# Seven products of sums in place of eight block products, in the query, key and gate projections of the first mixer

## The reference, cut to what matters

```python
h = rms_norm(x, norm_g[0])                  # 512 x 1024
proj = h @ a_w_in                           # 1024 x 4096
q, k, v, gate = jnp.split(proj, 4, axis=-1) # 16 heads of 64
# 2-D neighbourhood attention of q, k, v with a bias table, then
return (o * jax.nn.silu(gate)) @ w_out
```

## Time and profile before

| what | us |
|---|---|
| runs | 1197.37, 1195.59, 1196.95; median 1196.95 |
| span of the profiled execution, first to last instruction | 1194.2 |
| v stage, first matmul of half 9 to first of half 0 | 39.69 to 73.89 |
| q, k and gate stage, on PE | 73.89 to 208.37 |
| first DVE instruction of the attention's `frontA` | 210.05 |
| PE busy, share of the span | 95% |

### The profile page before, as it was taken

One profiled execution on the slowest core, in us unless ns is written; L12 is line 12 of the kernel. 1 busy time (PEld: TensorE's weight loads), 2 busy tenths in 40 slices (PEclk: granted clock), 3 DMA queues, 4 the chain that ended last, 5 costly groups with the idle time before them and its releaser, 6 DMA issues.

```text
span 1194.2 us, 24820 instructions
## 1 busy us (share of the span) xinstructions
PE 1136.4 (95%) x10359; PEld 953.4 (80%) x10359; DVE 588.2 (49%) x1304; ACT 516.5 (43%) x1041; POOL 417.7 (35%) x363
## 2 busy tenths in 40 slices
PE   3999999899999999999999999998999999999996
PEld 2988888799998998656699999876777887687863
DVE  5000001862427247788623338118865896335546
ACT  4232222973424432498734356244873522133321
POOL 5734574776335446300253335230014350000000
PEclk9999999999999999999999999989999999999998
DMA  7432342323221323200032224342002232100001
GB/s 219 147 104 74 106 115 96 98 73 82 73 87 54 107 71 106 71 1 2 5 138 72 72 71 148 120 131 63 2 2 71 71 106 89 54 22 4 3 3 71
DMA packets 73337, 89.60 MB, mean 75 GB/s; under 512 B 2017, under 2 KB 66666, under 8 KB 73098
## 3 DMA queue, kind: packets, MB, share of 16 engines
q1 hardware_dynamic: 70136, 78.12, 20.4%
q0 software_dynamic: 2416, 8.26, 2.8%
q10 hardware_dynamic: 674, 1.64, 0.5%
HBM read 83.75 MB, written 4.26 MB: 74 GB/s over the span
## 4 chain that ended last, share of the span: by engine, by line
PE 83%; DVE 8%; ACT 5%; issue 2%; POOL 1%; DMA 1%; ACTq 1%; DVEq 0%; POOLq 0%
PE bank L477 76%; PE bank L804 2%; ACT arena L1380 2%; PE bank L1003 1%; POOL ring_parts L2699 1%; PE bank L714 1%; ACT arena L1496 1%; PE bank L569 1%; ACT arena L1761 1%; DVE arena L1933 1%; DMA vrow<-in_final_norm_g 1%; DVE stat L1922 1%; DVE arena L2426 0%; ACT ring_parts L1409 0%; ACTq L1375 0%
## 5 line engine op out<-in xcount | busy, mean ns | idle before, releaser
L2699 POOL TENSOR_TENSOR ring_parts<-ring,ring_parts 128x512 fp32r<-128x512 f32 (+1 forms) x236 | 309.2, 1342 | 431.1 <-ACT ring_parts L1409 339.5
L477 PE MATMUL bank<-ring_parts,arena_parts 128*128 128x256 f32 x1856 | 320.4, 282 | 0.0
L477 PEld LDWEIGHTS bank<-ring_parts,arena_parts 128*128 128x128 f32 x1856 | 269.9, 189 | 1.6 <-issue 1.2
L477 PE MATMUL bank<-hT_parts,ring_parts 128*128 128x512 f32 x704 | 235.4, 396 | 0.0
L477 PE MATMUL bank<-arena_parts,ring_parts 128*128 128x512 f32 x640 | 225.3, 402 | 2.8 <-POOL ring_parts L2699 2.8
L477 PE MATMUL bank<-ring_parts,hT_parts 128*128 128x256 f32 x1024 | 219.9, 282 | 3.8 <-POOL ring_parts L2699 2.9
L1380 ACT ACTIVATE arena<-bank 128x512 f32<-128x512 f32 (+5 forms) x295 | 139.8, 541 | 189.5 <-PE bank L477 185.6
L477 PE MATMUL bank<-arena 64*64 64x64 f32 (+7 forms) x2288 | 177.4, 301 | 7.2 <-ACT arena L1380 2.4
L477 PEld LDWEIGHTS bank<-ring_parts,hT_parts 128*128 128x128 f32 x1024 | 169.4, 189 | 5.0 <-POOL ring_parts L2699 3.7
L477 PEld LDWEIGHTS bank<-arena 128*64 128x64 f32 (+3 forms) x2288 | 119.7, 145 | 53.0 <-issue 19.4
L477 PEld LDWEIGHTS bank<-hT_parts,ring_parts 128*128 128x128 f32 x704 | 133.5, 190 | 32.0
(11 more groups left out here) (273 smaller groups left out, 1397.5 us busy)
## 6 DMA issues: line engine op xcount, KB each, us to landing
ring<-in_a_w_in SPq DMA_DIRECT2D x16, 1024.0 KB, 5.5
ring<-in_w_in SPq DMA_DIRECT2D x15, 1024.0 KB, 5.5
ring<-in_b_w_in SPq DMA_DIRECT2D x10, 1024.0 KB, 5.2
ring<-in_ple_w_gate SPq DMA_DIRECT2D x8, 1024.0 KB, 5.1
arena<-rpb_rows POOLq DMA_DIRECT2D x16, 256.0 KB, 3.6
ring<-in_a_w_out SPq DMA_DIRECT2D x4, 1024.0 KB, 5.1
ring<-in_b_w_out SPq DMA_DIRECT2D x4, 1024.0 KB, 5.0
ring<-in_w_out SPq DMA_DIRECT2D x4, 1024.0 KB, 5.2
```

Of the source, the lines that this page charges most:

```text
L477: return nc.tensor.matmul(o, l, r, start=start, stop=stop)
L2699: nc.gpsimd.tensor_tensor(rounded(r), r, read_back(high_slot(n)[:, o:o + m // 4]), ALU.subtract)\
```

## The change

The twelve halves of q, k and gate (`SEVEN`) are no longer computed as 2x2x2 blocks (two halves of the 1024 inputs, two of the 256 outputs, two of the 512 tokens), but with seven products of sums of blocks, each of 12 matmuls of 256 columns.

- Three sums of token blocks (T1, T2, T4, each 128x1024) and a fourth in place (T3) are made by DVE straight after the token norm. Their high parts are ACT's (`high_sum`), their low parts POOL's (T1, T2, T4, between `lower(2)` and the bias of head 0) and DVE's (T3). They lie in the space of x, which SP loads again after the stage.
- Per half, DVE makes four sums of weight blocks of 128x512 (`sum_operand`) and two of the seven low parts (`low_operand`), ACT seven high parts of 128x512 (`high_operand`), POOL five low parts of 128x512.
- A ring of `NOP` = 6 operand pairs takes the place of the raw slot 3 and the two high slots; the raw ring has three slots in this stage.
- The outputs are combined on the way out of PSUM: per half, ACT copies two (`first_out`, `left_out`) and DVE makes four or five `scalar_tensor_tensor` from a bank and an SBUF tile (`second_out`, `third_out`, `last_out`). PE reuses a bank for products 4, 5 and 6, and product 5 waits for `third_out`.
- `lower(3)` moves behind the bias of heads 0 and 1; `lower` of `("AO", 0)` moves to head 8, into the attention stage; the high parts of `("AO", 0)` and `("AO", 1)` move from before the attention stage into its steps 1 and 2.
- Two small loads into `wa` move from POOL's start to behind `low_pair(0, 7)`.

```diff
 # tensor engine
-            for n in AORD:
+            for n in AORD[0:4]:
                 need3(("A", n))
...
+            def seventh(m, b, again=False):
+                h, q = divmod(m, 7)
+                if q in (4, 5):
+                    pe.wait_ge(S("A_low_v"), 2 * h + q - 3)
                 else:
-                    for s in range(2):
-                        fm3(("A", n, s), "a" if n < 8 else "v", ("A", n), s * P, act)
+                    pe.wait_ge(S("A_low_g"), 5 * h + min(q, 4) + 1)
+                left, right = (tuple(rounded(v) for v in pair) for pair in (operand(m), RIGHT[q]))
+                def one(a, c, k, st, sp):
+                    return nc.tensor.matmul(b[:, 0:256], left[a][:, k, :], right[c][:, k, :], start=st, stop=sp,
+                                            skip_group_check=again)
+                for k in range(4):
+                    one(0, 0, k, k == 0 and not again, False)
+                    one(0, 1, k, False, False)
+                    ins = one(1, 0, k, False, k == 3)
+                return ins
...
+            pe.wait_ge(S("A_tlow"), 3)
+            for h, n in enumerate(SEVEN):
...
+                end(seventh(m + 2, b6), ("A", n, "6"))
...
+                end(seventh(m + 3, b7), ("A", n, "7"))
+                evacuated(pe, ("A", n, "1"))
+                end(seventh(m + 4, b1, True), ("A", n, "11"))
+                evacuated(pe, ("A", n, "7"))
+                end(seventh(m + 5, b7, True), ("A", n, "21"))
+                pe.wait_ge(S("A_22"), h + 1)
+                end(seventh(m + 6, b5, True), ("A", n, "12"))
 # scalar engine
+            def high_operand(m):
+                h, q = divmod(m, 7)
+                if q in (1, 2, 3, 6):
+                    act.wait_ge(S("A_sum"), 4 * h + min(q, 4))
+                else:
+                    raw_here(act, first7 + h)
+                free_operand(act, m)
+                nc.scalar.activation(rounded(operand(m)[0]), source(m), ACT.Copy).then_inc(S("A_high"), 1)
...
+            high_operand(0)
+            high_operand(1)
...
+            for m in range(1, 7 * len(SEVEN) + 2):
+                h, q = divmod(m - 1, 7)
+                if q == 0 and h < len(SEVEN):
+                    first_out(h)
+                if q == 0 and h:
+                    tanh_a(h - 1, 1)
+                if q == 1 and h:
+                    tanh_a(h - 1, 0)
+                if q == 4:
+                    left_out(h)
+                if m + NOP - 1 < 7 * len(SEVEN):
+                    high_operand(m + NOP - 1)
...
-            high(HI[("AO", 1)])
...
                 if 1 <= j < 9:
                     ptA_copy(j - 1)
+                if j in (1, 2):
+                    high(HI[("AO", j - 1)])
 # vector engine
+            TT(T1[1], h_block(0, 1), h_block(0, 0), ALU.subtract).then_inc(S("A_tsum"), 1)
+            dve.wait_ge(S("A_tsum"), 1)
+            TT(T2[1], h_block(1, 1), T1[1], ALU.subtract).then_inc(S("A_tsum"), 1)
+            dve.wait_ge(S("A_tsum"), 2)
+            TT(T4[1], h_block(1, 0), T2[1], ALU.subtract).then_inc(S("A_tsum"), 1)
+            dve.wait_ge(S("lo_norm0"), 8)
+            TT(h_block(0, 1), h_block(1, 1), h_block(0, 1), ALU.subtract).then_inc(S("A_tsum"), 1)
...
+                if q == 1:
+                    raw_here(dve, first7 + h)
+                    s1 = weight_block(h, 0, 1)
+                    TT(s1, s1, weight_block(h, 1, 1), ALU.add).then_inc(S("A_sum"), 1)
+                    dve.wait_ge(S("A_sum"), 4 * h + 1)
...
+                    TT(s2_sum, s1, weight_block(h, 0, 0), ALU.subtract).then_inc(S("A_sum"), 1)
+                if q in (3, 6):
+                    free_operand(dve, m)
+                    dve.wait_ge(S("A_sum"), 4 * h + 2)
+                    TT(operand(m)[1], weight_block(h, 1, int(q == 3)), s2_sum, ALU.subtract).then_inc(S("A_sum"), 1)
...
+            def prepare(m):
+                sum_operand(m)
+                low_operand(m - 1)
...
+            for m in range(1, 7 * len(SEVEN) + 3):
+                h, q = divmod(m - 1, 7)
+                if q == 2:
+                    second_out(h)
+                if q == 3:
+                    third_out(h)
+                if q == 5:
+                    last_out(h, "21")
+                if q == 6:
+                    last_out(h, "12")
+                if m + NOP - 1 < 7 * len(SEVEN):
+                    prepare(m + NOP - 1)
...
+                if q == 0 and h:
+                    gate_a(h - 1, 1)
+                if q == 1 and h:
+                    gate_a(h - 1, 0)
 # gpsimd
-            lower(2, HI[("A", 12)])
+            lower(2)
+            for n, t in enumerate((T1, T2, T4)):
+                pool.wait_ge(S("A_thigh"), n + 1)
+                pool.wait_ge(S("A_tsum"), min(n + 2, 3))
+                nc.gpsimd.tensor_tensor(rounded(t[1]), t[1], read_back(t[0]), ALU.subtract).then_inc(S("A_tlow"), 1)
...
             for h in range(16):
                 if h == 2:
-                    lower(HI[("A", 12)] + 1)
+                    lower(3)
                 if h == 4:
-                    lower(HI[("A", 12)] + 2, HI[("AO", 0)])
+                    for m in range(7 * len(SEVEN)):
+                        if m % 7 not in (4, 5):
+                            pool.wait_ge(S("A_high"), m + 1)
+                            hi, lo = operand(m)
+                            nc.gpsimd.tensor_tensor(rounded(lo), source(m), read_back(hi), ALU.subtract)\
+                                .then_inc(S("A_low_g"), 1)
+                if h == 8:
+                    lower(HI[("AO", 0)])
 # sync engine
+                if n == HI[("AO", 3)]:
+                    sp.wait_ge(filled, J[("A", SEVEN[-1], "12")] + 1)
...
+                if n == HI[("AO", 3)]:
+                    for l in range(NT):
+                        sp.dma_start(x[:, l, :], A["x"][0].rearrange("(r c) d -> c r d", r=GR)[CT * l:CT * l + CT])\
+                          .then_inc(s_x[l], 16)
```

More of the change, by code:

```diff
@@ L47 @@
 NRAW, NHI = 4, 2
+NRAW7 = 3
+NOP = 6
 CH = 64
@@ new lines, in first_out, with left_out @@
+            def first_out(h):
+                n = SEVEN[h]
+                key = ("A", n, "1")
+                b = take(act, key)
+                if h >= 2:
+                    evacuated(act, ("A", SEVEN[h - 2], "21"))
+                give(copy(sums[:, h % 2, 0, :], b[:, 0:256], 0.125 if n < 4 else 1.0), key)
+            def left_out(h):
+                n = SEVEN[h]
+                key = ("A", n, "11")
+                b = take(act, key)
+                if n < 4:
+                    copy(qT[:, 2 * n, 0:192], b[:, 64:256], 0.125)
+                    give(copy(qT[:, 2 * n, 448:512], b[:, 0:64], 0.125), key)
+                elif n < 8:
+                    give(copy(kT[:, 2 * n - 8, 0:256], b[:, 0:256]), key)
+                else:
+                    give(copy(G[:, 2 * n - 24, 0:256], b[:, 0:256]), key)
@@ new lines, in _ @@
+            high_operand(0)
+            high_operand(1)
+            act.wait_ge(filled, half_last[3] + 1)
+            high_operand(2)
+            act.wait_ge(S("A_tsum"), 4)
+            nc.scalar.activation(rounded(T3[0]), block4(h_full, 0, 1, 256), ACT.Copy).then_inc(S("A_thigh3"), 1)
+            for m in range(3, NOP):
+                high_operand(m)
+            for m in range(1, 7 * len(SEVEN) + 2):
[10 more added lines that the diff above has]
+                    high_operand(m + NOP - 1)
@@ L1487, in expA @@
+            tanh_a(len(SEVEN) - 1, 0)
             def expA(j):
@@ L1986, in _, with h_block @@
             gain_tile("norm0", 3)
[L1988 to L1994 removed]
+            def h_block(kh, t):
+                return block4(h_full, kh, t, 256)
+            evacuated(dve, ("norm0", 3, 1))
@@ new lines, in low_operand, with second_out @@
+            def low_operand(m):
+                h, q = divmod(m, 7)
+                if q in (4, 5):
+                    dve.wait_ge(S("A_high"), m + 1)
+                    hi, lo = operand(m)
+                    TT(rounded(lo), source(m), read_back(hi), ALU.subtract).then_inc(S("A_low_v"), 1)
+            def second_out(h):
+                n = SEVEN[h]
+                key = ("A", n, "6")
+                b = take(dve, key)
+                evacuated(dve, ("A", n, "1"))
+                give(STT(sums[:, h % 2, 1, :], b[:, 0:256], 0.125 if n < 4 else 1.0, sums[:, h % 2, 0, :],
+                         ALU.mult, ALU.add), key)
+                evacuated(dve, key)
@@ new lines, in third_out, with last_out @@
+            def third_out(h):
+                n = SEVEN[h]
+                key = ("A", n, "7")
+                b = take(dve, key)
+                u = sums[:, h % 2, 0, :]
+                give(STT(u, b[:, 0:256], 0.125 if n < 4 else 1.0, sums[:, h % 2, 1, :], ALU.mult, ALU.add), key)
+                evacuated(dve, key)
+                out_a(n, 1, bank[slot[("A", n, "12")]], u, 256, 512).then_inc(S("A_22"), 1)
+            def last_out(h, name):
+                n = SEVEN[h]
```

(7 more changed lines are left out.)

181 lines of the change are left out of this document (136 added, 45 removed).

## The result

| | before | after |
|---|---|---|
| median of the runs, us | 1196.42 (4 runs, 1195.59 to 1197.37) | 1217.34 (4 runs, 1215.70 to 1217.97) |
| ratio, 95% interval | | 1.0168, 1.0153 to 1.0183 |
| span of the profiled execution | 1194.2 | 1215.9 |

The kernel is 1.7% slower; the forecast was 1206.0 with a range to 1213. The direction was right, the size was not. In spans, 12.7 us more were lost than the +9.0 forecast (1203.2 against 1215.9), and I look for them stage by stage.

The account below looks back on a forecast made before the run. PE, busy 95% of the span, was taken as the bound. A gain of -15.1 us and costs elsewhere summed to +9.0 on a span of 1194.2: 1203.2, plus 2.75 for the median, 1206.0 us; range 1196 to 1213.

Parts of the forecast that it names:

- The token sums, +3.6: After the token norm, DVE's sums and POOL's low parts hold each other up, making half 9 3.6 us later.
- The wait into the first product: PE stands from the last v matmul until drain, high part and low part are through: +2.5 us, bounds 2.2 and 2.9.
- The stall of each half: PE waits 0.6 us before product 5 for `third_out`, 0.85 in two gate halves; together +7.1 us, bounds 0 and 13.
- no exclusion: Rival: DVE and POOL don't hinder one another; 3.6, 2.5 (ring start) and 7.1 vanish, 1192.8 us; chance 0.13.
- the path is the bound: Product stage: DVE and POOL's shared path sets the pace, a half over 11 us; clock or path, 1208 to 1215, chance 0.23.
- ACT's high parts, +3.0: Two ACT high parts of 1.90 us enter attention steps 1 and 2, delaying PE by 3.0 us, seen at `scoresA(4)`.
- Half 11, +4.3: In the v stage, `lower(3)` stands behind POOL's token low parts and two biases: +4.3 us, bounds 3.3 and 5.3.
- PE's gain, -15.1: Product stage: 84 matmuls of 256 columns replace 48 of 512 per half, 9.94 for 11.20 us, over twelve halves.
- The start of the ring, +2.5: First 10 us of products: ACT, POOL and DVE fill an empty ring, delaying early products; +2.5 us, bounds 0 and 3.5.
- I take +1.0 us for both, bounds 0 and 3.5: Attention: POOL's four low parts before head 8, and bias loads slowed by the reload of x, cost 1.0 us together.
- Later stages, 0: From the end of attention to the end of the kernel: no change forecast, 0 us.
- PE's clock falls: Rival: idle times halve PE's clock, costing about 3 us each; 1209, with two 1212; clock or shared path, chance 0.23.

Follow-up runs that it names:

- experiment 5: Changed kernel, but DVE makes the token sums only after POOL has finished half 9's low parts, `lower(1)`: 1216.26 us, ratio 1.0166.
- experiment 7: Changed kernel, but POOL makes only a quarter of the low part of each half's operand 0: 1210.57 us, ratio 1.0114.
- experiment 6: Changed kernel, but DVE makes s1 and s2, the next half's sums, behind `third_out` and not ahead of it: 1208.78 us, ratio 1.0103.
- experiment 3: Changed kernel with the reload of x later and the output projection's first low parts behind all heads: 1212.02 us, ratio 1.0129.
- Experiment 9: Changed kernel with the moves of experiments 1, 2, 4, 5 and 6, and ACT's two high parts in steps 6 and 9: 1195.99 us against 1197.72 before.
- experiment 1: Changed kernel, but the reload of x waits for the transposes of step 6 in the attention stage: 1211.3 us, ratio 1.013.
- experiment 4: Changed kernel, but POOL makes half 11's low parts, `lower(3)`, ahead of the bias of heads 0 and 1: 1211.3 us, ratio 1.0127.
- experiments 2 and 3: Experiment 2: changed kernel, but POOL makes the output projection's first low parts behind head 15's bias, 1212.35 us, ratio 1.0129. Experiment 3 has its own line.
- experiment 10: Experiment 9's kernel, but `lower(2)` waits for DVE's first three token sums and head 3's bias moves inside the products: 1196.97 us against 1197.72 before.

## Why the prediction was right or wrong

**Right, shown.** The token sums, +3.6: measured 3.62, of which 0.3 is a later start of everything before them (POOL's low parts at 31.87 for 31.54); experiment 5 takes the rest out. The wait into the first product: 2.43 recorded for 2.5 (2.7 by the pace of the matmuls, 84.88 - 70.82 - 11.36).

The stall of each half: the order of instructions came out as written, s2 1.67 us for "about 1.7". With 10.08 as the free pace, the eleven halves from the first product 5 (95.11) to the last (212.99) hold 117.88 - 110.88 = 7.0 us of stall; the recorded idle times in them are 5.0, and the other 2.0 stand in no recorded idle time. The forecast's 7.1 counts the first half too, so 6.5 of it belong to these eleven: eight halves lost 0.58 each for 0.6, the two with gate products 1.1 each for 0.85, the last 0.1 for nothing. That the totals agree to 0.1 us is in part luck.

The rival "no exclusion" is out (in experiment 7 s2 falls from 1669 to 832 ns by median with most of one POOL instruction gone, and a half from 10.65 to 10.08), and so is "the path is the bound": a half is 10.65, not over 11, and in experiment 6 the same instructions of DVE and POOL fit into 10.08. POOL's low part that meets a sum of 128x512 takes 1754 ns by median, the others 1298: a sum costs it 0.46 us, near the 0.5 of the earlier trace rows. That agreement is better than its reading was: POOL's four low parts at 383.86 met not only the two low parts of DVE but also short DVE instructions with two SBUF inputs behind them (one of 128x256 took 1.49 us at 387.32, and 0.41 when it came again at 390.35), so the row does not price one low part by itself.

**ACT's high parts, +3.0: 2.7.** The sign that the forecast named is there: `scoresA(4)` starts 24.7 us after `identb` (242.51) where it was about 22.0, and experiment 3, without the two loads on POOL, still has a stage 2.7 longer. Experiment 9, with the high parts in other steps, brings that start to about 23.0, and the 1.0 us left there goes with the lower clock.

**Half 11, +4.3: measured 4.7.** The forecast had POOL's `lower(2)` at 5.06. DVE's s1 and s2 of the first half start as soon as their weights are there, at 45.49, and met it: 5.78. A term left out, 0.7. The three token low parts took 7.1 for 7.5, which gave 0.4 back, and the forecast's own terms add up to 4.5 (70.5 - 66.0) and not 4.3.

**PE's gain, -15.1: mis-sized, measured -13.4.** I took 84 x 0.1183 from the v stage, 1.42 us a product. Experiments 6 and 7 show a half without waits at 10.08, 1.44 a product: 12 x (11.20 - 10.08) = 13.4. The small loss comes twelve times and is 1.7 us.

**The start of the ring, +2.5 and the first half's 0.6: measured 3.0.** From 84.88 to 95.11 are 10.23 us for five products, 7.2 without waits. The end of the stage, +0.1: 0.4, on DVE. The gain (1.7), the stall of the later halves (0.5) and the end (0.3), less 0.1 here, make the 2.4 us by which the product stage missed.

**The step that failed: in the attention, "I take +1.0 us for both, bounds 0 and 3.5".** Measured 6.7 (74.4 - 67.7). I had seen both loads on POOL, its lack of spare time, and the reload that could slow the bias loads. I priced only the low parts, at 2 us (experiment 1 leaves 2.1), let exp and transposes hide most of that, and gave the delayed load nothing. The load for one head took 8.9 us from issue to use (223.03 to 231.89) where the page had 3.6 from issue to landing; POOL stood 5.03; the low parts took 5.16; that is 10.2 us of an engine without spare time. With one of the two, attention is 69.4 to 69.8, with both 74.4, with none 67.7. So about 3 us of the first 5 are hidden and none of the second. What hides them (the four bias tiles, the banks of the scores) is argued, not shown.

Four other traces have both loads and no edit of their own in this stage (experiments 4 to 7), but POOL waits for the load more or less long. The shortest wait and the longest (experiments 6 and 7):

```profile
224.54 0.86 POOL L3047 TENSOR_TENSOR arena<-arena,cst 128x256 f32<-128x256 f32 x1 [3.37 <-DMA arena<-rpb_rows]
```
```profile
228.91 0.85 POOL L3045 TENSOR_TENSOR arena<-arena,cst 128x256 f32<-128x256 f32 x1 [5.48 <-DMA arena<-rpb_rows]
```

With waits of 3.37, 4.38, 4.73, 5.03 and 5.48 us (experiments 6, 5, 4, the changed kernel, 7) the stage takes 72.8, 73.9, 74.1, 74.4 and 74.9: each us of POOL's wait is one us of the stage. The chain of the changed kernel's attention says the same. It lies on POOL and its loads from here until 262.6, and in experiment 3, as before the change, no row of POOL is in it:

```profile
238.38 5.16 POOL ring_parts L2971 x4
```

A fall of PE's clock is a rival here, since the granted clock was 0.50 from 251 to 254, behind the waits of 1.29 and 2.32 us. It costs nothing that shows: in experiment 6 the clock stayed at 1.00 through the stage, and its point lies on the same line. The upper bound of 3.5 was the real mistake: it should have been the whole 10.2 less what is hidden. With 1.0 in place of the 6.7, the time would have been 1211.6, inside the range.

**Later stages, 0: measured +4.3, not settled.** The code there is the same, and so is PE's idle time to within 2 us. Windows of the two kernels from the attention's end to the last instruction:

```profile
292.20:1215.90 923.70, 887.42 (x8698) 737.07 (x8696) 520.43 (x1068) 402.27 (x796) 251.42 (x189) 0.99 0.20 63
```
```profile
274.80:1194.20 919.40, 885.10 (x8698) 736.05 (x8696) 519.21 (x1068) 402.23 (x796) 251.00 (x189) 0.99 0.20 64
```

The first figures are the window's length and PE's busy time: of the 4.3 us, 2.3 are PE being busy longer on the same matmuls, 2.0 idle time. In the ten experiments, which share this code, the same stretch takes 919.4 to 924.2 us. The changed kernel and its ten experiments average 921.9, so about 1.8 of the 4.3 is the scatter of one execution against another; the other 2.5 rest on a single trace of before, the equal of the lowest of the eleven. Clock falls at other places go with the scatter: what the granted clock lacked of 1.00, summed over windows of 5 us, comes to 9.8 us in the traces of 919.4 and 920.2 and to 16.3 in that of 924.2. But it is 12.1 before and 13.2 after, so it explains about 1 us between these two. One wait is longer in all eleven: PE's for the load of `cmp_w_v`, 1.2 to 1.8 us for 0.8 before. The rest stays open.

**The clock.** The rival "PE's clock falls" did happen behind half 9's wait of 3.95 us, as these windows of the changed kernel (length, busy times of PE, PEld, DVE, ACT, POOL, granted clock) show:

```profile
44.00:45.00 1.00, 1.00 (x7) 1.00 (x7) 0.00 (x0) 0.00 (x0) 1.00 (x4) 0.50 0.69 209
...
40.00:50.00 10.00, 6.69 (x33) 6.69 (x34) 3.03 (x2) 2.75 (x3) 9.98 (x14) 0.66 0.69 225
...
80.00:90.00 10.00, 7.17 (x57) 6.62 (x55) 5.29 (x4) 4.75 (x10) 6.45 (x4) 1.00 0.00 0
```

In windows of 1 us the granted clock is 1.00 to 42, 0.76 in 42 to 43, 0.50 from 43 to 49, 0.82 in 49 to 50 and 1.00 from there; the 0.66 over the ten us is their mean. A granted 0.5 in the stage was one of the signs that would have made the forecast wrong. It came in the v stage and not in the products, where every window of ten us from 80 to 210 shows 1.00, and it was swallowed by half 11's wait for POOL, as the forecast said of such a fall. The other kind, behind half 11's wait, is missing from the changed kernel's trace but stands in those of experiments 2 and 3 (0.50 in 73 to 75 and from 71.5 to 77), whose first product starts 1.6 and 3.4 us later with the same code up to there.

## What to carry to other kernels

When work moves into a stage whose queue is already the tight one, sum what it adds (issue, the time of a load beside the heaviest transfers, here 8.9 us from issue to use, instructions) and take all of it as the upper bound; two delays that each cost little alone, here 2.1 and 1.7 us, can cost much more together, here 6.7. In an in-order queue, put the instruction that frees another engine's bank ahead of preparations for later work: here that order alone took 7.0 us out of a stage of 133. A saving on the busiest engine of 13.4 us was only level with the kernel before when five such orders were mended; with a sixth it was worth 0.17% (interval 0.04 to 0.3).

## What the hardware did that was not expected

A DVE instruction with two SBUF inputs, 1.22 us alone, took 9.00 to 9.03 us in three kernels while POOL ran five instructions without a pause, and POOL was not slowed at all; with POOL held back it took 1.22. In the changed kernel three sums of the same kind took 2.19 to 2.31 us beside POOL, whose `lower(1)` took 6.34 for 5.01: both engines lost time there. Which of the two starts first does not settle it. In experiment 5 the long sum is recorded as started at 42.43, ahead of POOL's low parts at 42.96, and it ended at 51.44, behind them; in the changed kernel the first sum, recorded at 31.76, 0.11 us ahead of POOL's low part at 31.87, took its 1.22. The loads that POOL was issuing when the long sum began (41.84 to 42.94) are not the cause: in experiment 10 the sum began during the same two issues and took 1.22. What decides between the 2.2 us and the 9.0 stays open.

The granted clock did not follow the length of the wait alone. After 2.43 us of waiting at 84.88 the changed kernel's window of 84 to 94 shows 1.00; after 2.44 at 81.33 in experiment 4 that of 80 to 90 shows 0.83. Experiment 1, whose code is the changed kernel's up to there, waited the same 2.43 and had 0.83 in 84 to 94.
